# A two-layer hybrid decoder step on one core: where the query matrices are loaded, and in which place the samples' experts are gathered

## The reference, cut to what matters

```python
q = (tb @ wq).reshape(blk, PEER_HEADS, PEER_D_KEY)
s1 = jnp.einsum('thd,hkd->thk', q[..., :half], keys[:, 0])
s2 = jnp.einsum('thd,hkd->thk', q[..., half:], keys[:, 1])
sc1, i1 = lax.top_k(s1, PEER_TOPK)
sc2, i2 = lax.top_k(s2, PEER_TOPK)
cand = (sc1[..., :, None] + sc2[..., None, :]).reshape(blk, PEER_HEADS, PEER_TOPK * PEER_TOPK)
...
sc, sel = lax.top_k(cand, PEER_TOPK)
idx = jnp.take_along_axis(cidx, sel, axis=-1)
g = jax.nn.softmax(sc.astype(jnp.float32), axis=-1)
act = jax.nn.gelu(jnp.einsum('thkd,td->thk', u[idx], tb), approximate=False)
wgt = (g * act.astype(jnp.float32)).astype(tb.dtype)
return jnp.einsum('thk,thkd->td', wgt, v[idx])
```

## Time and profile before

| | |
|---|---|
| median of 3 runs | 2261.51 us (2261.38 to 2264.46) |
| the profiled execution, its own time | 2266.77 us |
| its span | 2265.2 us |
| TensorE busy | 1940.2 us, 86% |
| VectorE busy | 1514.0 us, 67% |
| ScalarE busy | 461.0 us, 20% |
| GpSimd busy | 643.6 us, 28% |
| moved by DMA | 744.46 MB, mean 329 GB/s |
| of it from GpSimd's queue | 582.18 MB |
| from the queue of SP | 160.47 MB |

### The profile page before, as it was taken

One profiled execution on the slowest core, in us unless ns is written; L12 is line 12 of the kernel. 1 busy time (PEld: TensorE's weight loads), 2 busy tenths in 40 slices (PEclk: granted clock), 3 DMA queues, 4 the chain that ended last, 5 costly groups with the idle time before them and its releaser, 6 DMA issues. The chain is left out here.

```text
span 2265.2 us, 26903 instructions
## 1 busy us (share of the span) xinstructions
PE 1940.2 (86%) x9186; PEld 1114.5 (49%) x9186; DVE 1514.0 (67%) x3831; ACT 461.0 (20%) x1384; POOL 643.6 (28%) x598
## 2 busy tenths in 40 slices
PE   7999889998898777777699998999989987787875
PEld 5887667654454222222278876676534442222221
DVE  3555443767877888787445544438688788888874
ACT  2344210221112111111122532102211211111111
POOL 0001000334444354445200000003444444444441
PEclk9999999999999999999999999999999999999998
DMA  5447696699999999999654467947999999999995
GB/s 191 156 131 265 215 317 237 248 410 418 421 421 414 375 417 421 421 421 415 272 185 147 142 228 268 339 162 296 404 422 421 421 418 371 422 421 421 421 416 236
DMA packets 188196, 744.46 MB, mean 329 GB/s; under 512 B 16339, under 2 KB 76172, under 8 KB 117378
## 3 DMA queue, kind: packets, MB, share of 16 engines
q0 software_dynamic: 83296, 582.18, 62.9%
q1 hardware_dynamic: 104754, 160.47, 20.9%
HBM read 731.33 MB, written 11.46 MB: 328 GB/s over the span
## 5 line engine op out<-in xcount | busy, mean ns | idle before, releaser
L1102 PE MATMUL ps<-arena 128*128 128x512 f32 (+1 forms) x2112 | 1011.9, 612 | 239.9 <-DVE arena L1691 233.7
L2208 POOL DMA_INDIRECT arena<-in_peer_uv,arena x528 | 604.7, 1145 | 868.6 <-PE ps L1102 705.4
L1682 DVE CUSTOM_DVE_ANT_0 arena<-arena,h 128x1024 f32<-128x1024 f32 x512 | 627.3, 1225 | 236.2 <-DMA arena<-in_peer_uv,arena 227.3
L1102 PEld LDWEIGHTS ps<-arena 128*128 128x128 f32 (+1 forms) x2112 | 366.3, 187 | 848.5 <-DVE arena L1691 523.8
L490 PE MATMUL ps<-ht_tok,wring 128*128 128x264 f32 (+2 forms) x1728 | 382.1, 376 | 7.3 <-DMA wring<-in_w_in 3.7
L490 PEld LDWEIGHTS ps<-ht_tok,wring 128*128 128x128 f32 x1728 | 310.9, 190 | 76.5 <-issue 17.7
L2000 ACT ACTIVATE arena<-arena 128x1 f32<-128x1 f32 x528 | 105.9, 203 | 1027.6 <-DVE arena L1682 1026.5
L1691 DVE TENSOR_SCALAR arena<-consts,arena 128x128 f32<-128x128 f32 (+1 forms) x528 | 181.3, 343 | 18.9 <-ACT arena L2000 17.7
L490 PE MATMUL ps<-arena,wring 128*128 128x264 f32 (+2 forms) x512 | 91.7, 336 | 0.8 <-DVE arena L1456 0.8
L490 PEld LDWEIGHTS ps<-arena,wring 128*128 128x128 f32 x512 | 77.2, 191 | 10.2 <-DVE arena L1456 1.3
L2189 POOL DMA_DIRECT2D nrow<-in_norm_ffn x2 | 1.1, 533 | 252.8 <-PE ps L856 252.8
(11 more groups left out here) (324 smaller groups left out, 1766.2 us busy)
## 6 DMA issues: line engine op xcount, KB each, us to landing
arena<-in_pages SPq DMA_DIRECT2D x256, 272.0 KB, 4.8
wring<-in_w_in SPq DMA_DIRECT2D x38, 1024.0 KB
wring<-in_peer_wq SPq DMA_DIRECT2D x18, 1024.0 KB
arena<-in_peer_uv,arena POOLq DMA_INDIRECT x528
h<-in_state_ssm POOLq DMA_DIRECT2D x16, 512.0 KB, 5.0
out<-h POOLq DMA_DIRECT2D x16, 512.0 KB, 3.8
wring<-in_w_ssm_proj SPq DMA_DIRECT2D x8, 1024.0 KB
arena<-in_w_out SPq DMA_DIRECT2D x8, 1024.0 KB, 12.4
```

Of the source, the lines that this page charges most:

```text
L1102: last = pe.matmul(ps[0:outs, SUM_BANK[t] + half, :], diag[:, n % DIAGS, 0:outs], ring[:, HOME[n % RING], D_MODEL + half * 512:D_MODEL + ( ...
L1682: dve.tensor_tensor_reduce(ring[:, HOME[k], 0:D_MODEL], ring[:, HOME[k], 0:D_MODEL], tokens, 1.0, 0.0, ALU.mult, ALU.add, dots[:, column(n ...
L2208: pool.indirect_dma_start(ring[:, HOME[k], :], None, table, bass.IndirectOffsetOnAxis(ap=idx[:, TOPK * u + j:TOPK * u + j + 1], axis=0)).t ...
```

## The change

Three things change.

1. *Where and when the query matrices are loaded.* There are now nine loads per layer. Head 0's first goes where it went (`wq_home`). Head 1's goes into the room of the latents and rotary keys (`wq_latents`), once their last reader, the samples' mix, is done, and stays there for both tiles. Head 4's goes into `wq_home` after head 0's first queries; head 0's again into the free end of the shared buffer (`wq_spare`) after the last `heads_out`; head 2's and head 5's into the two blocks of `wring`; head 3's into the room of `qz` and `hr` (`wq_early`). Heads 6 and 7 are loaded into the blocks when the queries of heads 2 and 5 have been made. The rooms of the scores are permuted (`SCORE_ROOM`), since `wq_home` lies in the rooms that heads 2 to 5 had. VectorE clears `qz` only after head 3's queries (slot 40, a wait more).
2. *The order of the units.* The sample unit stands last, after both prompt tiles. The second prompt tile gets banks 6 and 7, the samples get 4 and 5 after the first tile.
3. *The last slots.* In the last 8 slots VectorE makes the diagonal of the slot before ahead of the dot product of this one. TensorE signals each of the last two products separately (`last_sums`), and all tile sums are made in two halves.

```diff
@@ -55,14 +55,14 @@
-UNITS = [(0, hh) for hh in range(P_HEADS)] + [(2, 0)] + [(1, hh) for hh in range(P_HEADS)]
-SAMPLE_UNIT = P_HEADS
+UNITS = [(t, hh) for t in range(2) for hh in range(P_HEADS)] + [(2, 0)]
+SAMPLE_UNIT = 2 * P_HEADS
 UNIT_SLOTS = [TOPK // 2 if t == 2 else TOPK for t, _ in UNITS]
...
 SLOTS = len(SLOT)
-TILE_FIRST = (0, P + TOPK // 2, P)
-TILE_LAST = (P - 1, SLOTS - 1, P + TOPK // 2 - 1)
-SUM_BANK = (4, 4, 6)
+TILE_FIRST = (0, P, 2 * P)
+TILE_LAST = (P - 1, 2 * P - 1, SLOTS - 1)
+SUM_BANK = (4, 6, 4)
@@ -274,6 +274,9 @@
 assert ARENA_PEER["wq0"][0] >= ARENA_ATT["ql"][0] and ARENA_PEER["wq0"][1] <= ARENA_ATT["ql"][1]
+share(ARENA_PEER, "wq_early", ARENA_PEER["qz"][0], DC * BLOCK)
+assert ARENA_PEER["wq_early"][1] <= ARENA_PEER["hr"][1]
+SCORE_ROOM = (0, 1, 6, 7, 2, 3, 4, 5)
 share(ARENA_ATT, "wout01", S1 + SLOT_COLS, 2 * DC * BLOCK)
@@ -324,11 +327,14 @@
         gate = gates[:, :].rearrange("p (c t) -> p c t", c=2 * DC)
-        lat = sb("lat", 3 * KV_LORA)[:, :].rearrange("p (t r) -> p t r", t=3)
-        kpe = sb("kpe", 3 * ROPE)[:, :].rearrange("p (t r) -> p t r", t=3)
-        latt = sb("latt", 2 * TOKENS)[:, :].rearrange("p (c t) -> p c t", c=2)
-        kpet4 = sb("kpet", TOKENS)
-        cqt = sb("cqt", 3 * TOKENS)[:, :].rearrange("p (c t) -> p c t", c=3)
+        latents, lat_cols = cut([("lat", 3 * KV_LORA), ("kpe", 3 * ROPE), ("latt", 2 * TOKENS), ("kpet", TOKENS), ("cqt", 3 * TOKENS)])
+        latroom = sb("latents", lat_cols)
+        of_latents = lambda name: latroom[:, latents[name][0]:latents[name][1]]
+        lat = of_latents("lat").rearrange("p (t r) -> p t r", t=3)
+        kpe = of_latents("kpe").rearrange("p (t r) -> p t r", t=3)
+        latt = of_latents("latt").rearrange("p (c t) -> p c t", c=2)
+        kpet4 = of_latents("kpet")
+        cqt = of_latents("cqt").rearrange("p (c t) -> p c t", c=3)
         nrow = sb("nrow", D_MODEL)
@@ -433,7 +439,11 @@
         idx = peer("idx").bitcast(I32)
-        wq0 = peer("wq0").rearrange("p (c n) -> p c n", c=DC)
+        by_chunk = lambda ap: ap.rearrange("p (c n) -> p c n", c=DC)
+        wq_home = by_chunk(peer("wq0"))
+        wq_latents = by_chunk(latroom[:, 0:DC * BLOCK])
+        wq_spare = by_chunk(shared[:, 2 * A_HEADS * TOKENS - DC * BLOCK:])
+        wq_early = by_chunk(peer("wq_early"))
         diag = peer("diag").rearrange("p (k d) -> p k d", k=DIAGS)
@@ -970,17 +980,30 @@
-                        if (hh, lo) == (0, 0):
-                            pe.wait_ge(sem("wq0_load"), 16)
-                            state["wq", hh] = wq0
-                        elif m == 0:
-                            state["wq", hh] = next_block(DC, BLOCK)
+                        if m == 0:
+                            if (hh, lo) == (0, 0):
+                                pe.wait_ge(sem("home_loads"), 16)
+                                state["wq", hh] = wq_home
+                            elif (hh, lo) == (1, 0):
+                                pe.wait_ge(sem("latents_load"), 16)
+                                state["wq", hh] = wq_latents
+                            elif hh == 0:
+                                pe.wait_ge(sem("spare_load"), 16)
+                                state["wq", hh] = wq_spare
+                            elif hh == 3:
+                                pe.wait_ge(sem("early_load"), 16)
+                                state["wq", hh] = wq_early
+                            elif hh == 4:
+                                pe.wait_ge(sem("home_loads"), 32)
+                                state["wq", hh] = wq_home
+                            elif hh > 1:
+                                state["wq", hh] = next_block(DC, BLOCK)
                         if (hh, m) == (2, 0):
...
                         wide.filled(product(ps[:, b, 0:hi - lo], lambda c: w[:, c, m * P:(m + 1) * P], lambda c: ht[:, c, lo:hi], DC))
-                        marks["q", hh] = wide.n
+                        marks["q", hh] = marks["q", hh, lo] = wide.n
@@ -1021,6 +1044,7 @@
                     aux.filled(last)
+                    marks["samples_mixed"] = aux.n
                     pe.wait_ge(sem("aux_free"), 4 + aux.n)
@@ -1044,6 +1068,7 @@
                         mla(m, P, TOKENS)
+                    marks["late_mla"] = aux.n
                     queries(1, 0, 0, P)
@@ -1095,14 +1120,17 @@
                             pe.wait_ge(sem("aux_free"), 4 + marks["x", 1])
-                        elif n == TILE_FIRST[1]:
+                        elif n == TILE_FIRST[2]:
                             pe.wait_ge(sem("tile_added"), 1)
...
                                              start=n in TILE_FIRST, stop=n in TILE_LAST, skip_group_check=True)
-                        last.then_inc(sem("slots_used"), 1)
+                            if n == SLOTS - 1:
+                                last.then_inc(sem("last_sums"), 1)
+                        if n < SLOTS - 1:
+                            last.then_inc(sem("slots_used"), 1)
@@ -1598,7 +1626,7 @@
                             dve.wait_ge(sem("scores_out"), SCORES_AT[hh, t])
-                            halves = [keysc[:, hh, t, half, :] for half in range(2)]
+                            halves = [keysc[:, SCORE_ROOM[hh], t, half, :] for half in range(2)]
                         else:
@@ -1694,9 +1722,13 @@
                         r = P if t < 2 else SAMPLES
-                        dve.wait_ge(sem("slots_used"), TILE_LAST[t] + 1)
-                        last = dve.tensor_tensor(x[0:r, t, :].rearrange("p (a d) -> p a d", a=2), x[0:r, t, :].rearrange("p (a d) -> p a d", a=2),
-                                                 ps[0:r, SUM_BANK[t]:SUM_BANK[t] + 2, :], ALU.add)
+                        if t != 2:
+                            dve.wait_ge(sem("slots_used"), TILE_LAST[t] + 1)
+                        for half in range(2):
+                            if t == 2:
+                                dve.wait_ge(sem("last_sums"), half + 1)
+                            last = dve.tensor_tensor(x[0:r, t, half * 512:(half + 1) * 512], x[0:r, t, half * 512:(half + 1) * 512],
+                                                     ps[0:r, SUM_BANK[t] + half, :], ALU.add)
                         last.then_inc(sem("tile_added"), 1)
@@ -1727,15 +1759,20 @@
                         elif n == 40:
+
+                            dve.wait_ge(sem("wide_free"), 4 + marks["q", 3])
                             then(dve.memset(qz.rearrange("p s c -> p (s c)"), 0.0))
...
                             ahead = best_experts(u + 1) if u + 1 < len(UNITS) else iter(())
-                        inputs(n)
+                        if n < SLOTS - TOPK // 2:
+                            inputs(n)
                         if n:
                             diagonal(n - 1)
+                        if n >= SLOTS - TOPK // 2:
+                            inputs(n)
                         if j == 0:
@@ -1748,11 +1785,11 @@
                             last.then_inc(sem("qz_ready"), 1)
-                        for t in (0, 2):
+                        for t in (0, 1):
                             if n == TILE_LAST[t] + 5:
...
                     diagonal(SLOTS - 1)
-                    tile_sum(1)
+                    tile_sum(2)
                     dve.wait_ge(sem("tile_added"), 3)
@@ -1974,7 +2011,7 @@
                         cols = slice(2 * P * tiles[0], 2 * P * (tiles[-1] + 1))
-                        scored_bank(act.copy(keysc[:, hh, tiles[0]:tiles[-1] + 1, :, :].rearrange("p t s n -> p (t s n)"), ps[:, b, cols]))
+                        scored_bank(act.copy(keysc[:, SCORE_ROOM[hh], tiles[0]:tiles[-1] + 1, :, :].rearrange("p t s n -> p (t s n)"), ps[:, b, cols]))
@@ -2132,11 +2169,28 @@
                     w_q = of_layer("peer_wq", layer).rearrange("k p (c n) -> k p c n", c=DC)
-                    sp.dma_start(wq0, w_q[0]).then_inc(sem("wq0_load"), 16)
-                    first = count[0]
-                    assert first == marks["wq_block"]
-                    for k in list(range(1, P_HEADS)) + [0, 1]:
-                        load_block(w_q[k], DC, BLOCK)
+                    sp.dma_start(wq_home, w_q[0]).then_inc(sem("home_loads"), 16)
+
+                    sp.wait_ge(sem("lat_stores"), 64)
+                    sp.wait_ge(sem("aux_full"), marks["samples_mixed"])
+                    sp.dma_start(wq_latents, w_q[1]).then_inc(sem("latents_load"), 16)
+
+                    sp.wait_ge(sem("wide_full"), marks["q", 0, 0])
+                    sp.dma_start(wq_home, w_q[4]).then_inc(sem("home_loads"), 16)
+
+                    sp.wait_ge(sem("aux_full"), marks["heads", 1])
+                    sp.dma_start(wq_spare, w_q[0]).then_inc(sem("spare_load"), 16)
+
+                    assert count[0] == marks["wq_block"]
+                    load_block(w_q[2], DC, BLOCK)
+
+                    sp.wait_ge(sem("aux_full"), marks["late_mla"])
+                    sp.dma_start(wq_early, w_q[3]).then_inc(sem("early_load"), 16)
```

(5 more changed lines are left out.)

## The result

The changed kernel took 2234.05 us (median of 3 runs, 2233.46 to 2234.79) against 2261.51 (2261.38 to 2264.46): ratio 0.9875, 95% interval 0.9852 to 0.9897. That is 1.2% less, where 2.0% was forecast: 17 us above the forecast and 3 above the range. The profiled executions differ by more, 2265.2 to 2233.2 us of span, since that of before lay 5.3 us above its median.

The account below looks back on a forecast made before the run. The bytes the DMA engines carry in the expert gathers, and their idle time, were taken as the bound. Per layer 9.95 + 1.8 + 1.7 + 6.85 + 2.0 = 22.3 us, two layers 44.6: 2217 us, range 2208 to 2231.

Parts of the forecast that it names:

- Part 1's four loads: Four query-matrix loads leave the steady gather units, each saving 2.49 us: 9.95 us a layer.
- Rival A: In the first tile TensorE becomes the bound and half of Part 1's 11.75 us is lost: 2229 us, chance 0.15.
- Part 3: Moving the sample unit last removes GpSimd's 12.05 us idle gap between the prompt tiles: 6.85 us a layer, bounds 0 and 7.0.
- The unit of 39.76 us: One second-tile unit of 16 gathers, taken as the steady cadence of 2.485 us a gather.
- Part 1's fifth load: The load at 490, where TensorE and VectorE catch up, leaves the gathers: 1.8 us a layer, bounds 0 and 2.49.
- the 6.1: Time from a gather's issue to its use after a queue restart: 3.1 us to start, 2.5 to move, 0.5 to be seen.
- Part 2: Before the first expert sum, TensorE's wait for head 1's matrix goes: 1.7 us a layer, bounds 0 and 1.8.
- rival D: In the gather stage TensorE's clock falls to 1.2 GHz and slows slots; 40 such a layer make 2313 us, chance 0.03.
- Part 4: At the layer's end, one slot's matmuls and a half sum follow the last dot product: 2.0 us less, bounds 1.2 and 2.4.

Follow-up runs that it names:

- after_again: The changed kernel itself, unchanged, run once more: 2233.66 us, ratio 0.9873.
- head1_late: The changed kernel with head 1's matrix loaded where it was before, in front of head 2's: 2236.16 us, ratio 0.9880.
- gap3: The changed kernel with the gather of slot 136 held back until three slots more are summed: 2240.34 us, ratio 0.9887.
- gap5: The changed kernel with the gather of slot 136 held back until five slots more are summed: 2250.91 us, ratio 0.9944.
- order_alone: The kernel before with only the samples' unit moved to the end, with its banks: 2263.05 us, ratio 0.9998.
- loads_alone: The kernel before with only the change's weight loads (rooms, order, waits): 2243.92 us, ratio 0.9916.
- spread: The changed kernel with the second tile's choice of experts begun eight slots sooner and spread evenly: 2233.83 us, ratio 0.9877.
- vector_time: The kernel spread with one longer VectorE instruction more in each of slots 136 to 255: 2238.42 us, ratio 0.9881.
- fifth_true: The changed kernel with head 4's matrix loaded again among the gathers, at the time of the load taken away: 2232.95 us, ratio 0.9872.
- tail_alone: The kernel before with only the change's tail (earlier diagonals in the last eight slots, sums in halves): 2261.09 us, ratio 0.9982.

## Why the prediction was wrong, step by step

**Right: what bounds the kernel, and Part 1's four loads.** Slots 32 to 128, 254.6 us before and 245.1 after (244.6 in after_again): 9.4 to 9.9 us a layer for 9.95. Rival A did not come. The first gathers did not suffer either: five loads ahead of them, and the first rows are used 6.87 us after the issue for 7.85 (7.60 and 7.85 in head1_late).

**Wrong, the largest: Part 3**, "so 50 x (420 - 363)/420 = 6.8 us are lost". The bytes were missing, and the gap went, but the stage behind slot 128 became only 1.8 us shorter (345.5 to 343.7), 5 us a layer less than forecast. The step that failed is the one from missing bytes to lost time, and with it the silent assumption that the rest of the second tile would run as before. Two things stood in its place. At the gap the rows lost only 3.1 us where the bytes lost 6.4; gap3 and gap5 lose 1.4 to 2.8 us less than their bytes too. And 1.3 us of the 3.1 came back later.

That is the other side of the bytes: in the changed kernel the time missing is 6.5 us in the 275 us behind the first 50, where it was 1.3, so that the sum over the stage went from 8.2 to 7.0 us only. In windows cut in the same way the new order alone has 6.5 (order_alone) and the new loads alone 1.3 (loads_alone), and gap3 and gap5 bring it down to 2.0 and 3.3. So a gap makes the stream behind it run fuller. One explanation is that the 16 DMA engines are unevenly behind, that a gather is there when its last packets are, and that a gap lets the slowest catch up. The trace has no row for a single engine, so this is argued, not shown.

Over 135 slots the changed kernel's rows need 8.2 us more than 2.485 each, about eight skips of 1 us. In spread and vector_time each skip stands behind an instruction fetch, 28 of 28, and the distance moved with VectorE's instructions: so these are VectorE's fetches. The Trainium skill (Runtime: NRT & Kernel Launch, "Instruction fetch mechanics") says that an engine's next instructions are fetched while it executes the present ones and that the cost is mostly hidden. For VectorE itself the trace agrees: at the late row it waits 1.24 us for the gather's DMA and not for an instruction; it is the gathers that pay. Why VectorE's fetches delay them and SyncE's do not stays open. The unit of 39.76 us, read as the cadence, had such a fetch in it and no skip; it stood behind the gap that the change took out. The changed kernel's units take 40.8 us.

**Wrong: Part 1's fifth load**, "I take 1.8". It is 0: fifth_true has it back at no cost. TensorE sets the pace there, and the DMA engines had room for it. The bound 0 was named; the choice went by the gather's 7.8 us against the 6.1 that it was thought to need. The first gather behind gap5's gap took 5.5 us (784.30 to 789.83), but one at this place took 7.8 in the changed kernel (505.29 to 513.12) with no load beside it, so nothing was to be had.

**Partly wrong: Part 2**, 1.7 us. The wait went as said. But slots 0 to 17 became 0.2 us longer and slots 17 to 32 no shorter. A fall of TensorE's clock, which came with the early load in 31 of 32 layers, costs 1.3 us there, so most of the 1.7 is accounted for if the early load brings it about; it is rival D's mechanism in one place. Of the rest nothing is seen at slot 32.

**Part 4** was right: 2.6 us in layer 0 and 2.05 in layer 1 for 2.0.

The sum per layer from slot 0 to 263, by the table: 9.4 (slots 32 to 128) + 1.8 (128 to 263) - 0.2 (0 to 17) = 11.0 us. With the ends that is 2 x 11.0 + 2.6 + 2.05 = 26.7 us, against 27.5 between the medians, and 44.6 forecast. The two profiled executions differ by 32.0; the 5.3 us over these 26.7 lie ahead of slot 0, where before was among the slowest of all (419.0 us in layer 1, 414.2 in the changed kernel) and tail_alone, with the same code there, took 412.3.

## What to carry to other kernels

A gap in a stream's bandwidth is worth what its consumer loses, read from the last row before to the first steady row behind and then at the end of the stage, and not its missing bytes; put gaps of known size in before taking one out. Take the cadence from many units, not from one that stands behind a gap, and ask what skips it. A load costs its transfer only where the gathers set the pace: the same megabyte was 2.4 to 2.5 us in slots 32 to 128, 1.9 at 504 and nothing at 492.

## What the runs showed of the hardware

A fetch of 8 KB of VectorE's instructions set back the rows of a saturated gather stream by about 1 us (28 of 28 in spread and vector_time), 7 to 8 us a layer, but not behind a gap in the stream (before, 861.5; gap3, 862.8 and 907.6), and 16 more of SyncE's a layer did nothing. With TensorE's wait for head 1 gone (1.53 us in head1_late, 1.78 before) its granted clock fell (to 0.74 over 5 us in the changed kernel) some 27 us later in 31 of 32 layers, and in 3 of 8 with the wait; such a fall cost 1.3 us.
